# One stage for the first output projection, the norm and the routing, with expert slots found on chip

## The chip, the cores and the metric

The kernel runs on one NeuronCore of a Trainium2 chip. The metric is the device time of one execution in microseconds (us). Three runs of the kernel before took 3424.74, 3426.91 and 3428.15 us; their median is 3426.91 us. Everything is float32.

## The reference, cut to what matters

The model has two blocks; the change lies in the first one, between its attention and its mixture of experts. `x` is 512 tokens by 1024 features.

```python
x = x + concatenate([out_na, out_dil, out_mem], -1) @ w_out          # the first output projection
t = rms_norm(x, g_ffn)                                               # norm before the experts
grp_logits  = t @ w_r1 + b_r1                                        # 4 groups
fine_logits = (t @ w_r2 + b_r2).reshape(n, 4, 8)                     # 8 experts in a group
grp_idx = argmax(grp_logits); grp_gate = softmax(grp_logits)[grp_idx]
top_val, top_idx = top_k(fine_logits[:, grp_idx], 2)
gate = grp_gate * softmax(top_val)
y[token] += gate * ((silu(t @ w1[e]) * (t @ w3[e])) @ w2[e])         # for both experts e of a token
x = x + y
```

There are 32 experts, each with two 1024 x 512 matrices and one 512 x 1024 matrix, 6 MB together. 512 tokens with two experts each make 1024 rows, 32 rows to an expert in the mean.

## The kernel before, in words

The program is a row of stages. In a stage each engine has a list of instructions of its own, ordered by semaphores, and a stage begins only when every engine has ended the one before it, its awaited DMAs included. The helper `link` in the routing puts a wait for each VectorE instruction behind it, so a chain of small operations runs one after the other.

The stages around the change are, in order:

- `project_out` (L1117), stage `out1`. For each of 4 tiles of 128 tokens TensorE multiplies 8 chunks by 2 halves of `first_w_out` (L1203) and VectorE adds the bank to `x_rows` (L1263). Meanwhile SyncE asks for the weights of experts 0 and 1 (`experts.load_gate`, `load_up`, `load_down`, L239, L243, L247). The last of them, the down weights of expert 1, waits for the end of the products, since the attention's output lies in its place.
- `load_tiles` (L930), stage `in_ffn`: the norm weights, once by feature and once as a row copied to all partitions.
- `norm_and_turn` (L960), stage `norm_ffn`: squares and sums (L1017, L1052), root (L1021), inverse (L1063), scaled rows (L1027, L1068), 32 transposes (L1100), copies with the norm weights (L1036, L1077) into `hT`, the rows times the weights (L1086), and their store to the DRAM tensor `scr_tokens` (L1003).
- `route` (L1771). SyncE loads the router weights and constants (L1825) and then 17 tiles for the filter work described below (L1827). TensorE makes 36 logits a token (L1835). VectorE picks the group and the two experts in a chain of small operations (L1893 to L1923, the sum of the two one-hot choices is `both`). TensorE counts the earlier rows of each expert (L1843) and all rows (L1847). VectorE turns that into a slot number a row (L1951 to L1959), and GpSimd scatters the row's information to the DRAM tensor `scr_slot_info`, 8 indirect DMAs one after the other (L1977). An expert owns 64 slots; rows beyond 64 go to further blocks.
- `experts_stage` (L2333), stage `moe`. SyncE reads the slot table back (L2367). For each expert GpSimd gathers 64 rows from `scr_tokens` (L2322), TensorE transposes them (L2288), ScalarE copies the transposed rows (L2457), TensorE makes both up products (L2298), ScalarE and VectorE the gated activation (L2474, L2497), TensorE the down product (L2315), VectorE copies it (L2488) and GpSimd scatters the rows (L2329). SyncE asks for the gate weights of expert b + 2 when the first up product of expert b is done (L239), for its up weights when the second is done (L243), and for the down weights of b + 1 when the down product of b - 1 is done (L247). Two experts' weights fit on chip.
- Between these products runs `FilterWork` (L2009), which makes the spectra of long filters that a later layer needs. A fixed plan gives each of its pieces one of three slots an expert (`SLOTS`, `HID0`, `SUMS` and others), and every engine runs its part of the piece at that slot.
- `rest_stage` (L2503) computes the blocks beyond the first 64 rows of an expert, if there are any, and `combine_experts` (L2734) adds the gated rows to `x_rows`.

The order on VectorE in `experts_stage` is: filter piece 3b, the activation of b, filter piece 3b + 1, the copy of the down product of b - 1, filter piece 3b + 2. On ScalarE the copy of the transposed rows stands behind the SiLU:

```python
nc.scalar.activation(act1[:], ph1[:, 0:HF], ACT.Silu).then_inc(s_silu, 1)
filters.on_scalar(act, nc.scalar, n_slots * b)
if b + 1 < E:
    copy_x(b + 1)
```

## Time and profile before

| | |
|---|---|
| median of 3 runs | 3426.91 us |
| the profiled execution's own time | 3431.24 us |
| its span, first to last instruction | 3429.5 us |
| TensorE busy | 3035.7 us, 89% of the span |
| VectorE, ScalarE, GpSimd busy | 31%, 21%, 5% |
| mean granted TensorE clock | 0.947 of full |
| moved by DMA | 442.48 MB |
| stage `out1` begins | 461.8 us |
| stage `moe`: first DMA asked for, last product ends | 597.65 us, 1168.0 us |

Times in the rows are us from the start of the span. In a row of the timeline the first number is the start, the second the duration, and the bracket says how long the engine was idle before and what released it. PE is TensorE's matmuls, PEld its weight loads, DVE VectorE, ACT ScalarE, POOL GpSimd, SPq the queue of DMAs that SyncE issues. A float32 matmul of the program shows as two records, a transpose as one.

### The profile page before, as it was taken

The page shows a single profiled execution, that of the slowest core. Times are in us where ns is not written, and L with a number is a line of the kernel's source. Part 1 is how long each engine was busy: PE and PEld are TensorE (multiplying, and loading weights), DVE is VectorE, ACT ScalarE, POOL GpSimd, SP SyncE. Part 2 cuts the span into 40 slices and gives each one's busy share as a digit, 9 for nine tenths or more (in the row PEclk, how much of TensorE's full clock was granted, in tenths as well). Part 3 has the DMA queues.
Part 4 walks back from the last instruction along what each step waited for, and adds up shares of the span by engine and source line. Part 5 has one row for each costly group of instructions (what it writes and reads, how often), then busy time and mean ns, then how long its engine had stood idle before and what let it go on. Part 6 is the DMA issues. An engine that isn't in the chain of part 4 may idle for free. (4 is left out here: it accounts for less than half of the span.)

```text
span 3429.5 us, 34727 instructions
## 1 busy us (share of the span) xinstructions
PE 3035.7 (89%) x13906; PEld 1814.0 (53%) x13906; DVE 1051.1 (31%) x2186; ACT 732.2 (21%) x1603; POOL 164.3 (5%) x265
## 2 busy tenths in 40 slices
PE   6999993899899589899989899989997776888998
PEld 3448653555444275567545566445654343454674
DVE  3441623212211210125421037333311872201242
ACT  2111621111010020234220048310001110202441
POOL 0000000111011000000000002001110001000000
PEclk9999995899999899999999999999999887999999
DMA  6664344899999801120001220012224213011200
GB/s 217 239 227 169 136 172 119 309 387 389 386 391 387 315 19 49 37 74 1 25 0 37 62 87 2 1 55 86 88 88 142 74 62 122 0 55 52 71 1 25
DMA packets 246599, 442.48 MB, mean 129 GB/s; under 512 B 31503, under 2 KB 113439, under 8 KB 243116
## 3 DMA queue, kind: packets, MB, share of 16 engines
q1 hardware_dynamic: 234150, 403.96, 33.5%
q0 software_dynamic: 9776, 22.18, 1.9%
q10 hardware_dynamic: 2518, 14.16, 1.0%
q8 instruction: 110, 1.80, 0.2%
q14 instruction: 45, 0.37, 0.0%
HBM read 410.04 MB, written 37.81 MB: 131 GB/s over the span
## 5 line engine op out<-in xcount | busy, mean ns | idle before, releaser
L352 PE MATMUL hyena_in_main<-hT,weight_slots 128*128 128x256 f32 (+1 forms) x1024 | 330.5, 486 | 1.4 <-PEq L993 1.4
L352 PEld LDWEIGHTS hyena_in_main<-hT,weight_slots 128*128 128x128 f32 x1024 | 194.5, 190 | 137.2 <-issue 124.0
L2298 PE MATMUL moe_ph<-expert_weights,moe_x_T 128*64 128x256 f32 x2048 | 239.8, 388 | 23.9 <-DMA expert_weights<-w 15.0
L2298 PEld LDWEIGHTS moe_ph<-expert_weights,moe_x_T 128*64 128x64 f32 x2048 | 145.8, 139 | 133.1 <-issue 44.8
L352 PE MATMUL swa_in_main<-hT,weight_slots 128*128 128x512 f32 (+1 forms) x576 | 190.8, 491 | 6.8 <-DMA weight_slots<-b_w_in 5.4
L352 PE MATMUL mla_down_main<-hT,weight_slots 128*128 128x512 f32 (+1 forms) x448 | 168.5, 539 | 19.5 <-DMA weight_slots<-a_w_in 19.5
L1412 PE MATMUL qkv_main<-hT,weight_slots 128*128 128x512 f32 (+1 forms) x384 | 167.8, 580 | 0.9 <-PEq L993 0.9
L1203 PE MATMUL post_y<-expert_weights,hT 128*128 128x512 f32 x384 | 165.1, 592 | 0.0
L352 PEld LDWEIGHTS swa_in_main<-hT,weight_slots 128*128 128x128 f32 x576 | 110.4, 192 | 87.6 <-issue 74.7
L352 PE MATMUL mla_up_main<-expert_weights,weight_slots 128*128 128x512 f32 (+1 forms) x416 | 146.4, 511 | 2.8 <-PEq L993 2.4
L352 PEld LDWEIGHTS mla_down_main<-hT,weight_slots 128*128 128x128 f32 x448 | 88.1, 198 | 100.0 <-issue 75.0
L1203 PE MATMUL post_y<-expert_weights 128*128 128x512 f32 x320 | 137.7, 592 | 0.0
L2315 PE MATMUL moe_py<-expert_weights,moe_act_T 128*64 128x512 f32 x512 | 118.6, 606 | 4.5 <-DMA expert_weights<-w 4.5
L1203 PEld LDWEIGHTS post_y<-expert_weights,hT 128*128 128x128 f32 x384 | 73.0, 190 | 92.0 <-issue 92.0
L1412 PEld LDWEIGHTS qkv_main<-hT,weight_slots 128*128 128x128 f32 x384 | 71.1, 190 | 92.4 <-issue 85.8
L860 DVE TENSOR_REDUCE mla_att_stat<-mla_att_scores 128x1 f32<-128x768 f32 (+1 forms) x80 | 68.1, 851 | 165.7 <-PE mla_att_scores L802 154.3
L1473 DVE RECIPROCAL expert_weights<-expert_weights 128x512 f32<-128x512 f32 (+1 forms) x24 | 77.3, 3220 | 133.6 <-ACT expert_weights L1446 133.6
L352 PEld LDWEIGHTS mla_up_main<-expert_weights,weight_slots 128*128 128x128 f32 x416 | 78.8, 190 | 69.7 <-issue 64.5
L352 PE MATMUL mla_down_main<-weight_slots,hT 128*128 128x256 f32 x512 | 111.0, 379 | 2.8 <-PEq L993 2.8
L786 PE MATMUL mla_att_scores<-mla_kn,expert_weights 128*128 128x512 f32 (+1 forms) x288 | 107.1, 490 | 3.0 <-ACT weight_slots L900 1.5
L1217 ACT ACTIVATE post_squares<-post_y 128x512 f32<-128x512 f32 x44 | 26.3, 598 | 372.2 <-PE post_y L1203 371.5
L352 PEld LDWEIGHTS mla_down_main<-weight_slots,hT 128*128 128x128 f32 x512 | 97.1, 190 | 16.3 <-issue 3.2
(361 smaller groups left out, 4101.5 us busy)
## 6 DMA issues: line engine op xcount, KB each, us to landing
expert_weights<-w SPq DMA_DIRECT2D x96, 2048.0 KB, 21.8
first_w_out<-w_mod SPq DMA_DIRECT2D x12, 2048.0 KB, 8.1
expert_weights<-w_mod SPq DMA_DIRECT2D x12, 2048.0 KB, 8.1
weight_slots<-w_in SPq DMA_DIRECT2D x16, 1024.0 KB
weight_slots<-c_w_in SPq DMA_DIRECT2D x16, 1024.0 KB
weight_slots<-a_w_in SPq DMA_DIRECT2D x14, 1024.0 KB
expert_weights<-scr_spectra SPq DMA_DIRECT2D x12, 1024.0 KB, 4.9
weight_slots<-b_w_in SPq DMA_DIRECT2D x10, 1024.0 KB
```

The source lines that it names most:

```text
L352: mm = pe.matmul(main[u][0:unit.rows, 0:unit.cols], lhsT, rhs, start=(c == 0), stop=(c == r.kc - 1))
L786: mm = pe.matmul(region[e][:, b0:b1], qn[:, 2 * it.pair + e, it.q], kn[:, 2 * it.pair + e, it.first + b0:it.first + b1], start=start, stop ...
L860: nc.vector.tensor_reduce(sm[:, MX, e:e + 1], region[e][:, 0:it.keys], AX.X, ALU.max)\
L1203: mm = pe.matmul(y[k % 4][:, half * BANK:(half + 1) * BANK], z_T[:, c, s.at + t * P:s.at + (t + 1) * P], w_sb[:, c, half * BANK:(half + 1) ...
L1217: nc.scalar.activation(junk[:], y[k % 4][:, half * BANK:(half + 1) * BANK], ACT.Square, accum_out=stat[:, k, half:half + 1]).then_inc(s_sq, 1)
L1412: mm = pe.matmul(main[n % B][:, 0:u.cols], lhsT, rhs, start=(c == 0), stop=(c == KD - 1))
L1473: nc.vector.reciprocal(rt, rt).then_inc(s_inv, 1)
L2298: mm = pe.matmul(bank[half * T:(half + 1) * T, 0:HF], x_T[:, c, :], w[:, c, half * HF:(half + 1) * HF], start=(c == 0), stop=(c == KD - 1))
L2315: mm = pe.matmul(py[half * T:(half + 1) * T, :], act_T[:, c % per, c // per * T:(c // per + 1) * T], w[:, c, half * BANK:(half + 1) * BANK ...
```

## The change

The stages `out1`, `in_ffn`, `norm_ffn` and `route` become one stage, `front`:

- TensorE: after the products of tile k come the transposes of tile k - 1 and the logits of tile k - 2. VectorE adds tile k, ScalarE squares and sums it, takes the root, VectorE inverts it, and the two scale one half of the row each; both copy half of the transposed rows.
- The norm weights are no longer applied to the rows. They are multiplied once into the router weights, and in the expert stage into the gathered rows as these are copied. The row copy of the norm weights and the stage that loads it are gone.
- The slot table in DRAM is gone for the 32 own blocks. A one-hot matrix of slot numbers (128 rows by 128 slots, for each of 8 tile and choice pairs) is multiplied with the one-hot expert choices times the row's number, which gives each slot its row: `expert_slots` on chip. The 8 indirect DMAs and the table move to `rest_stage`, inside its branch.
- GpSimd gathers the rows of experts 0 and 1 in the new stage, into one tile of 128 partitions whose halves take turns.
- SyncE's order is: 13 constants, gate and up weights of experts 0 and 1, 9 filter tiles, the four stores of `scr_tokens`, down weights of expert 1, down weights of expert 0 (its place holds the scaled rows until they are stored).
- 8 filter tiles (3.8 MB: two halves of `filter_w`, the lag row, the decay table, four cosine and sine tables) are now asked for at the start of `experts_stage`, ahead of the weights of expert 2. The filter plan's `SUMS` moves from slot 3 to slot 6 and waits for them.
- In `experts_stage` the copy of the transposed rows moves from ScalarE to VectorE, with the norm weights as a second operand, between the activation and filter piece 3b + 1.
- The gates, the further blocks and their experts are computed after the slots are found.

Tiles that were allocated inside the second block are now allocated earlier, without other effect. The core of the diff:

```diff
+    def gather(self, pool, b):
+        at = slice(b % 2 * SLOTS_B, (b % 2 + 1) * SLOTS_B)
+        gather_rows(pool, self.rows[at, :], self.tokens, self.index[0:SLOTS_B, b, 0:1]).then_inc(self.gathered[b % 2], 16)
...
+def out_and_route(nc, a, x, hT, routed, experts, consts, room, more, beside):
...
+                for tile, src in loads:
+                    sp.dma_start(tile, src).then_inc(s_in, 16)
+                for e in range(experts.EARLY):
+                    experts.load_gate(sp, e)
+                    experts.load_up(sp, e)
+                for tile, src in beside:
+                    sp.dma_start(tile, src).then_inc(s_beside, 16)
+                for k in range(XT):
+                    for half in range(2):
+                        sp.wait_ge(s_normed[half], k + 1)
+                    sp.dma_start(routed.tokens[k * P:(k + 1) * P, :], normed[:, k, :]).then_inc(s_tok, 16)
+
+                sp.wait_ge(s_y, XT)
+                experts.load_down(sp, 1)
...
+                sp.wait_ge(s_tok, 16 * XT)
+                experts.load_down(sp, 0)
...
+                for k in range(XT):
+                    if k >= 2:
+                        pe.wait_ge(s_x, k - 1)
                     for j in range(KD):
...
+                    mm.then_inc(s_y, 1)
+                    if k:
+                        turn(k - 1)
+                    if k >= 2:
+                        logits(k - 2)
+                logits(XT - 2)
+                turn(XT - 1)
+                logits(XT - 1)
 
                 pe.wait_ge(s_hot, 1)
...
+                pe.matmul(pre[:, 0:XT * E], consts["earlier"][:], flat, start=True, stop=False, skip_group_check=True)
+                for k in range(1, XT):
+                    mm = pe.matmul(pre[:, k * E:XT * E], consts["ones"][:], flat[:, 0:(XT - k) * E],
+                                   start=False, stop=(k == XT - 1), skip_group_check=True)
...
+                for k in range(2 * XT):
+                    pe.wait_ge(s_slot_hot, k // XT + 1)
+                    mm = pe.matmul(slot_of[:, 0:E], slot_hot[:, k, :], tagged[:, k, :], start=(k == 0), stop=(k == 2 * XT - 1))
...
+                link(tt(tagged, hots, c["result_no"].rearrange("p (k o) -> p k o", o=1).to_broadcast([P, 2 * XT, E]),
+                        ALU.mult))
...
+                link(v.tensor_reduce(rank, picked, AX.X, ALU.add))
...
+                    tt(slot_hot[:, at, :], slot_no, rank[:, at, :].to_broadcast([P, XT, P]), ALU.is_equal)\
+                        .then_inc(s_slot_hot, 1)
...
+                link(v.tensor_scalar(f["empty"], tag, 0.5, float(UNUSED), ALU.is_lt, ALU.mult))
+                link(v.scalar_tensor_tensor(f["base"], tag, -1.0, f["empty"], ALU.add, ALU.add))
+                link(v.tensor_scalar(f["second"], tag, X + 0.5, -float(X), ALU.is_gt, ALU.mult))
+                link(tt(f["token"], f["base"], f["second"], ALU.add))
+                v.tensor_copy(routed.index[:, :, 0], f["token"]).then_inc(s_index, 1)
...
-    HID0, SIN0, HID1, SIN1, SUMS, FIRST = 2, 4, 5, 7, 3, 9
+    HID0, SIN0, HID1, SIN1, SUMS, FIRST = 2, 4, 5, 7, 6, 9
...
-                with nc.allow_non_contiguous_dma(reason="an index a row, a block to a column"):
-                    for dst, src in loads:
-                        sp.dma_start(dst, src).then_inc(s_idx, 16)
+                filters.load(sp)
...
-                    if b + 1 < E:
-                        copy_x(b + 1)
...
+                def copy_x(b):
+                    dve.wait_ge(s_px, b + 1)
...
+                    nc.vector.tensor_tensor(x_T[b % 2][:], px[:].rearrange("p (c n) -> p c n", n=SLOTS_B),
+                                            routed.gain[:].rearrange("p (c o) -> p c o", o=1)
+                                            .to_broadcast([P, KD, SLOTS_B]), ALU.mult).then_inc(s_xT, 1)
```

## Rows read from the trace of the kernel before

**Rows 1.** The page's 40 slices of 85.7 us: tenths busy, GB/s moved

```profile
PE   6999993899899589899989899989997776888998
GB/s 217 239 227 169 136 172 119 309 387 389 386 391 387 315 19 49 37 74 1 25 0 37 62 87 2 1 55 86 88 88 142 74 62 122 0 55 52 71 1 25
```

**Rows 2.** Windows: stretch, length, busy us per engine (instructions), PEclk, DMA share, GB/s

```profile
517.00:546.80 29.80, 5.89 (x32) 5.26 (x32) 13.00 (x17) 8.82 (x12) 0.00 (x0) 0.65 0.42 158
...
585.40:597.65 12.25, 0.00 (x0) 0.00 (x0) 0.00 (x0) 0.00 (x0) 7.75 (x8) 0.50 0.02 1
...
616.50:1168.00 551.50, 520.33 (x3354) 274.29 (x3348) 115.31 (x181) 55.08 (x121) 59.41 (x60) 0.99 1.03 383
```

**Rows 3.** Waits of PE from 616 to 1168: us in total, times, longest

```profile
PE moe_ph L2298 <- DMA expert_weights<-w: 15.0, 10, 5.6
...
PE moe_py L2315 <- DMA expert_weights<-w: 4.5, 4, 1.8
PE moe_px L2288 <- DMA moe_x<-scr_tokens,moe_index: 3.3, 6, 0.9
```

**Rows 4.** Timeline of the last head, the output projection and the norm

```profile
441.25 1.09 PE L571 MATMUL heads_turned<-const_identity,ctx_rows_and_rope 128*128 128x128 f32 x8
...
461.81 20.41 PE L1203 MATMUL out_y<-first_w_out,expert_weights 128*128 128x512 f32 x47 [0.63 <-PEq L535]
...
475.82 1.22 DVE L1263 TENSOR_TENSOR x_rows<-out_y,x_rows 128x1024 f32<-128x1024 f32 x1 [17.45 <-PE out_y L1203]
...
517.02 1.22 DVE L1263 TENSOR_TENSOR x_rows<-out_y,x_rows 128x1024 f32<-128x1024 f32 x1 [12.51 <-PE out_y L1203]
...
526.32 1.06 ACT L1017 ACTIVATE norm_ffn_squares<-x_rows 128x1024 f32<-128x1024 f32 x1 [64.81 <-PEq L935]
```

**Rows 5.** Timeline of the routing and of the first expert

```profile
553.10 13.87 PE L1835 MATMUL route_logits<-route_w,hT 128*128 128x36 f32 x64 [15.15 <-DMA route_slot_info<-slot_info]
...
567.24 0.17 DVE L1893 TENSOR_REDUCE route_gmax<-route_logit 128x4 f32<-128x16 f32 x1
...
573.78 0.29 DVE L1923 TENSOR_TENSOR route_both<-route_hot 128x128 f32<-128x128 f32 x1
...
584.32 0.17 DVE L1959 CAST route_slots<-route_dest 128x8 int32<-128x8 f32 x1
...
597.65 2.00 SPq L2367 DMA_DIRECT2D moe_index<-scr_slot_info  x2
...
603.46 0.97 POOL L2322 DMA_INDIRECT moe_x<-scr_tokens,moe_index  x1 [8.17 <-DMA moe_index<-scr_slot_info]
...
606.60 3.67 PE L2288 MATMUL moe_px<-const_identity,moe_x 64*128 64x64 f32 x16 [24.57 <-DMA moe_x<-scr_tokens,moe_index]
...
616.55 0.37 SPq L239 DMA_DIRECT2D expert_weights<-w  x1
...
619.89 2.00 PE L2288 MATMUL moe_px<-const_identity,moe_x 64*128 64x64 f32 x16
```

**Rows 6.** Windows of the filter tiles' loads: stretch, length, PEclk, DMA share, GB/s

```profile
554.00:558.00 4.00, 0.50 0.98 346
558.00:570.00 12.00, 0.50 1.05 209
570.00:574.00 4.00, 0.50 0.97 273
```

**Rows 7.** Weight stream's start: window of 20 to 60 us into the experts

```profile
620.00:660.00 40.00, 39.23 (x274) 0.96 1.05 387
```

**Rows 8.** An expert's copy of the gathered rows, the next product, VectorE's price

```profile
664.89 0.60 ACT L2457 ACTIVATE moe_x_T<-moe_px 128x512 f32<-128x512 f32 x1 [6.94 <-PE moe_px L2288]
...
670.34 3.67 PE L2298 MATMUL moe_ph<-expert_weights,moe_x_T 128*64 128x256 f32 x32
...
L2241 DVE TENSOR_TENSOR hT<-moe_filter_banks,ctx_rows_and_rope 128x512 f32<-128x512 f32 x48 | 30.9, 686 | 50.0 <-PE moe_filter_banks L2160 50.0
...
L2213 DVE TENSOR_TENSOR filter_w<-filter_w,weight_slots 64x2048 f32<-64x2048 f32 x2 | 4.6, 2282 | 0.0
```

More of the change, by code:

```diff
@@ L67 @@
 class Stage:
[L71 removed]
+    POOLS = ((99, 166), (166, 232))
     turn = 0
@@ new lines, in out_and_route @@
+    with Stage(nc, "front") as st:
+        z_T, w_out = consts["z_T"], consts["w_out"]
+        normed = experts.W2_flat(0).rearrange("p (t n) -> p t n", n=D)
+        squares = hT[:, 0:XT, X:TOK]
+        w, b = more.tile(KD, R), st.sb("b", [P, R])
+        c = {k: more.tile(P) if k == "slot_no" else st.sb(k, shape)[:] for k, shape in ROUTE_CONSTS.items()}
+        sums, root, inv = (st.sb(k, [P, XT]) for k in ("sums", "root", "inv"))
+        t = {k: room.tile(XT, n) for k, n in dict(
+            logit=R, gmax=1, geq=E_GROUPS, gcand=E_GROUPS, gidx=1, ghot=E_GROUPS, gexp=E_GROUPS, gsum=1, ggate=1,
+            off=E_GROUPS, fine=E, v1=1, eq1=E, cand1=E, i1=1, fine2=E, v2=1, eq2=E, cand2=E, i2=1,
+            both=E, diff=1, ratio=1, one=1, p1=1, p2=1).items()}
+        hots, tagged, picked, slot_hot = room.tile(2 * XT, E), room.tile(2 * XT, E), room.tile(2 * XT, E), room.tile(2 * XT, P)
+        t["hot1"], t["hot2"] = hots[:, 0:XT, :], hots[:, XT:2 * XT, :]
+        rank, over_at, under = room.tile(2 * XT, 1), room.tile(2 * XT, 1), room.tile(2 * XT, 1)
+        found = {k: more.tile(E) for k in ("second", "empty", "base", "token", "row")}
+        jump = more.tile(E)
+        count, blocks, end = st.sb("count", [E, 1]), st.sb("blocks", [E, 1]), st.sb("end", [E, 1])
+        over, blocks_wide, ended = st.sb("over", [E, X // SLOTS_B]), more.tile(P)[0:E], st.sb("ended", [E, REST + 1])
@@ new lines, in logits @@
+                def logits(k):
+                    for half in range(2):
+                        pe.wait_ge(s_copied[half], k + 1)
+                    if k == 0:
+                        pe.wait_ge(s_w, 1)
+                    for j in range(KD):
+                        mm = pe.matmul(lg[:, k * R:(k + 1) * R], hT[:, j, k * P:(k + 1) * P], w[:, j, :],
+                                       start=(j == 0), stop=(j == KD - 1), skip_group_check=True)
+                    mm.then_inc(s_lg, 1)
+                pe.wait_ge(Stage.out_in, Stage.out_loaded)
@@ L2116, in begin, with load @@
         self.s_lag_in = st.sem("next_lag0_in")
+        self.s_loaded = st.sem("filter_constants_in")
+        self.n_loads = 16 * len(self.loads())
+    def load(self, sp):
+        for tile, src in self.loads():
+            sp.dma_start(tile, src).then_inc(self.s_loaded, 16)
     ARG_STEPS = 6
```

522 lines of the change are left out of this document (280 added, 242 removed).

## The prediction

> **What bounds the kernel now.** I read the page's slices first. TensorE is busy nine tenths nearly everywhere, but slices 6 and 7 (514 to 600 us) fall to 7 and 3 tenths, and right behind them the moved bytes stay at some 388 GB/s for six slices [rows 1]. So there is a gap, and then a stretch that runs at the pace of the DMAs.
>
> The windows by stage say the same. From 517 to 546.8 us TensorE works 5.9 us, and from 585.4 to 597.65 not at all; from 616.5 to 1168 it is busy 520 us, the DMA engines' share is 1.03 and 383 GB/s move [rows 2]. In that stretch TensorE waits 15.0 and 4.5 us for expert weights and 3.3 us for gathered rows [rows 3]. The busy share would point to TensorE, the waits to the weights: the product in front of a wait is late only because its weights are, and the queue never runs dry. I take the expert stage as a weight stream of fixed length. It begins when SyncE may ask for the gate weights of expert 2, at 616.55, behind the first up product [rows 5]. All that the change saves is then how much earlier this request comes, less what is put in front of the stream.
>
> The timeline gives the path to that request. Products begin at 461.81 and the last tile is added from 517.02 [rows 4]; then norm, logits from 553.10 to 567.0, a VectorE chain from 567.24 to 584.5, eight scatters, the table read back from 597.65, a gather from 603.46 to 606.60, transposes, a copy, the first up product [rows 5]. From first product to request: 616.55 - 461.81 = 154.7 us.
>
> **The same path after the change, term by term.**
>
> 1. *Products.* Unchanged, 517.02 - 461.81 = 55.2 us [rows 4].
> 2. *Work put between them.* Before the products of tile 3 end, TensorE also runs two groups of 8 transposes and one group of logits. Eight transposes take 1.1 us [rows 4]. A group of logits is 16 records; at the low clock 64 took 13.87 us, 3.5 a group, and at the full clock 16 records of the same kind of weight load took 2.0 [rows 5]. TensorE will be at the full clock here, as it comes from long products, so 2.0; both ends go to the range. Sum 4.2 us.
> 3. *Tile 3.* VectorE's add 1.2 and ScalarE's squares 1.1 [rows 4], and I put 1.0 for accumulator read, root, inverse and their hand-overs, 0.6 for scaling half a row (half the elements of the add or the square). ScalarE then scales before it copies its half of tile 2, another 0.6 (a 512-wide copy) [rows 8]; TensorE does the logits of tile 1 meanwhile and then waits for that copy to do those of tile 2 (2.0), transposes tile 3 (1.1), waits for a 512-wide copy on VectorE (0.7) [rows 8] and does the last logits (2.0). Sum 10.4 us.
> 4. *Choice of group and experts.* From 567.24 to the end of `both` at 574.07 is 6.8 us [rows 5]. Two small operations leave the chain (-0.4), and one add of all logits comes before it (+0.4), with 0.2 for the hand-over: 7.0 us.
> 5. *From `both` to the comparison with slot numbers.* TensorE does 8 records of counts and 8 of prefixes, where it now has 20 of prefixes and 8 of counts. The engine has been idle by then for 7 us; at such a place the clock is at the low level (0.50) [rows 2], so 0.22 us a record [rows 5], a bit less for the narrow counts: 2.5 us. VectorE then needs two products of 128 elements (0.3 each), a sum over 256 (0.45) and the first comparison of 512 (0.69) [rows 5, 8]. The second comparison lies beside the slot products: 16 records at 0.22 = 3.5 us. With hand-overs 8.0 us.
> 6. *Slots to indices.* Five operations of 32 columns, each near 0.17 and 0.04 behind it [rows 5]: 1.1 us. Here the two gathers may start: 3.1 us from issue to use [rows 5]. They are hidden behind term 7.
> 7. *Rest of the chain.* Index column, jumps, further blocks, gates: some 23 small operations of VectorE with one trip to ScalarE and back, 5.4 us by the same 0.2 each and a few of 256 elements at 0.45. Before, the gates lay beside TensorE's prefixes; now the stage's end waits for all of them. The next stage starts 0.3 us later, 461.81 against the end of the one before. Sum 5.7 us.
> 8. *First expert.* Transposes to request now take 616.55 - 606.60 = 9.95 us [rows 5]. The copy is 0.69 in place of 0.60 [rows 8]: 10.1 us. The clock is low at the start as before.
>
> Sum: 55.2 + 4.2 + 10.4 + 7.0 + 8.0 + 1.1 + 5.7 + 10.1 = 101.7 us. The request comes 154.7 - 101.7 = **53.0 us earlier**. In these 53 us lie the DRAM table (584.5 to 603.5, 19 us), the wait for the norm weights and the stage bounds, and most of the norm and the logits.
>
> **Queues that work is moved past.** SyncE issues 13 constants before the weights; the first up products come 90 us later, so this costs nothing. The four token stores stand behind 8 MB of weights and 1.1 MB of filter tiles, some 25 us of traffic; the last store is asked for only at about 525, when that is done. The two down weights follow, 4 MB or 11 us, over by about 540. If all that were late it would be the gather that waits, at 548.
>
> **What is put in front of the stream.** Eight filter tiles, 3.8 MB, are asked for as the expert stage begins. Before, they shared 20 us with a further megabyte of filter tiles, part at 346 GB/s, part at 209 although the engines' share was 1.05, part at 273 [rows 6]. By place in the queue the decay table (1.5 MB) is the fast part, the 64-partition halves of the filter weights (2.1 MB in all) the slow one, of which now 1.05 MB are left, and the tables the third (1.3 MB). So 4.3 + 5.0 + 4.6, about 13.5 us, from 1.5 us into the stage: done 15 us in. The weights' traffic would otherwise begin at 10.1 + 1.7 = 11.8 us in (their first bytes come about 1.7 us behind the request). The stream is at its full rate from its start [rows 7], so the 3.2 us are lost to it. All at 209 GB/s would be 18 us and 8 lost; if they slip into gaps, none. I take 3.2.
>
> **The move of the copy to VectorE** adds 32 x 0.69 = 22 us to 115 of 551 us [rows 2]. I cost it at nothing: VectorE has ended the activation, 0.4 us behind the second up product, when the transposes (2.0 us) end, and the copy is not wanted before the down product is over: 670.34 - 665.49 = 4.9 us of room at a typical expert [rows 8]. What stands behind it on VectorE, a filter piece and the copy of the down product, waits for TensorE anyhow. If that cover is gone, TensorE loses what the copy is later than 4.9 us. ScalarE loses 19 us of work, which frees nobody.
>
> A rule speaks against such a move. The Trainium skill, "SBUF — State Buffer", section "SBUF: two separate sides", says that a two-port VectorE operation locks GpSimd out of writing descriptors. By it the gathers would be late and the waits of rows 3 would grow. Its page "VectorE: DVE Perf Modes", "Why PSUM operands drop a tier", excludes PSUM operands from that mode, and this copy reads PSUM. No run here shows either yet.
>
> For the logits the skill's "TensorE: Matmul & The Clock Gate", section "LDWEIGHTS", gives columns / 1.2 ns, an estimated 1.7 us a group, not the 2.0 taken; by it the forecast would be about 1 us lower.
>
> **The sum.** 53.0 - 3.2 = 49.8 us gain. The profiled execution took 3431.24 us; 3431.24 - 49.8 = 3381.4. The median of the runs shown is 4.3 us below that execution, so the forecast for the median is **3377 us**.
>
> **The rivals.**
>
> *A. Less gain.* The terms come out at their dear ends: all logits at the low clock (+6, of which some 5 on the path), the filter tiles at 209 GB/s (+5), the tile pipeline of term 3 and the tail some 2 longer. Gain 38, time 3389. For it: the small loads' rates [rows 6]. Against: the clock was full through the products. Chance 0.24.
>
> *B. More gain.* TensorE's clock stays high to the slot products (24 records at half the price, -2.5), the filter loads find gaps (-3.2). Gain 55.5, time 3371. Against: the low clock between sparse products [rows 2]. Chance 0.16.
>
> *C. Slower.* The copy on VectorE becomes the link of the expert loop: VectorE stands in its order at a filter piece or the activation when the transposes end. Price: over 31 experts it has to eat 49.8 us and 7 more, 1.8 us each, so the copy must end 6.7 us behind today's. It decides from 4.9 us on. At 6.9 us late the time is 3377 + 31 x 2.0 = 3439. For it: filter work of up to 4.6 us in one go [rows 8]. Against: this comes once or twice, and VectorE is busy a quarter. Chance 0.02.
>
> *D. No change.* The stream isn't what ends the stage, or the rows beyond 64 slots exist after all and the table is still made (here no instruction of that stage shows, and the choice is computed as before). Then part of the gain is lost; all of it only if something unseen holds the stage's end, 3427. Chance 0.02.
>
> **How the numbers follow.** The forecast's own case, gain 45 to 54, has 0.56. A and B lie on the same side. The range goes from B with a further 5 us of earlier stream, 3366, to A with 4 us more, 3393; beyond it lie C, D and the tails of A and B, under 0.2. A change of 0.2% (7 us) is about what a measurement of this kernel can tell from none. Faster by more than that: 0.56 + 0.24 + 0.16 = 0.96; within: D, 0.02; slower: C, 0.02.
>
> **What the profile after should show.** Right: last tile added near 521; last logits ending near 531.5; indices near 548; first gather issued there; first transposes of the expert stage near 553.5; request for expert 2 near 563.5; down product of the last expert ending near 1118; the DMA share at 1.03 to 1.04 in between and stage `moe` from that request on 3 us longer than 551.5. Wrong: if TensorE's waits for expert weights grow to tens of us with a share below 1.0, the stream isn't the bound; if waits for VectorE's `moe_x_T` appear at each expert, C; if the stage from its request to the end is shorter by more than a few us, I misread the bound.

## The result, and the profile after

The changed kernel takes **3378.43 us** (median of 4 runs, 3378.07 to 3378.99) against 3426.43 us of the kernel before in the same comparison: 48.0 us less, ratio 0.986 (95% interval 0.9846 to 0.9874). Its profiled execution has its own time of 3378.07 us and a span of 3376.4 us. The forecast was 3377 us with a range of 3366 to 3393.

The page's slices of the changed kernel (the same two lines as [rows 1], slices of 84.4 us):

```profile
PE   6999997999999488999989999989997776888998
GB/s 219 235 236 164 150 180 208 385 385 390 388 389 385 183 44 38 35 66 1 26 13 47 54 76 2 1 74 88 87 90 140 63 84 103 13 44 53 72 1 25
```

The one slice at 3 tenths (514 to 600 us before) is one at 7 now, and its neighbour has 9 instead of 8. The stretch at 385 to 390 GB/s begins one slice sooner; before, it was five slices at 386 to 391 with partly filled ones on both sides. It is as high as before: the stream has not become faster, it starts earlier.

Windows of the changed kernel (length, busy time per engine with instructions, granted clock, DMA share, GB/s), the front stage and then the stretch from the request for expert 2's gate weights to the end of the last down product:

```profile
517.00:546.80 29.80, 19.19 (x103) 16.88 (x102) 12.66 (x42) 4.53 (x7) 0.00 (x0) 0.63 0.44 159
566.30:1118.00 551.70, 523.66 (x3342) 275.26 (x3340) 136.27 (x212) 36.78 (x90) 58.66 (x60) 0.98 1.03 384
```

Beside [rows 2], TensorE works 19 of 29.8 us where it worked 5.9, and the expert stage has the same share and rate. VectorE is busy 136 us there instead of 115, ScalarE 37 instead of 55: the moved copy. TensorE's waits in the expert stage (us in total, times, longest), to be held against [rows 3]:

```profile
PE moe_py L2462 <- DMA expert_weights<-w: 11.1, 7, 1.8
PE moe_ph L2445 <- DMA expert_weights<-w: 8.0, 9, 1.3
...
PE moe_px L2436 <- DMA gathered_rows<-scr_tokens,expert_slots: 2.5, 3, 1.1
```

19.1 us for weights where there were 19.5, and 2.5 for gathered rows where there were 3.3. The waits are those of a stage that is still paced by its weights; the first group of experiments tests that.

Now the timeline. The last tile, from its add to the last logits:

```profile
519.63 1.23 DVE L1994 TENSOR_TENSOR x_rows<-front_y,x_rows 128x1024 f32<-128x1024 f32 x1 [12.95 <-PE front_y L1901]
...
520.30 1.87 PE L1891 MATMUL front_logits<-weight_slots,hT 128*128 128x36 f32 x16
...
523.94 2.90 PE L1891 MATMUL front_logits<-weight_slots,hT 128*128 128x36 f32 x16 [1.77 <-ACT hT L1939]
...
526.65 1.95 PE L1881 MATMUL front_turned<-const_identity,expert_weights 128*128 128x128 f32 x8
...
529.38 3.60 PE L1891 MATMUL front_logits<-weight_slots,hT 128*128 128x36 f32 x16 [0.78 <-ACT hT L1939]
...
533.02 0.31 DVE L2005 TENSOR_TENSOR ctx_rows_and_rope<-front_logits,front_b 128x144 f32<-128x144 f32 x1 [4.54 <-PE front_logits L1891]
```

The same group of 16 logits records takes 1.87, 2.90 and 3.60 us, and 8 transposes 1.95 instead of 1.04. The clock by windows says why: 1.00 from 519 to 523, 0.93 from 523 to 525, 0.50 from then on. Behind it, the chain to the slots, the gathers and the first expert:

```profile
539.90 0.42 DVE L2038 TENSOR_TENSOR ctx_rows_and_rope<-ctx_rows_and_rope,front_result_no 128x256 f32<-128x256 f32 x1
...
544.23 3.62 PE L1929 MATMUL front_slot_of<-ctx_rows_and_rope 128*128 128x32 f32 x16 [1.01 <-DVE ctx_rows_and_rope L2056]
...
548.79 0.18 DVE L2064 CAST expert_slots<-weight_slots 128x32 int32<-128x32 f32 x1
...
549.97 1.37 POOL L2469 DMA_INDIRECT gathered_rows<-scr_tokens,expert_slots  x1 [507.44 <-DVE expert_slots L2064]
...
551.64 0.96 POOL L2469 DMA_INDIRECT gathered_rows<-scr_tokens,expert_slots  x1 [0.30 <-issue]
...
553.92 0.24 DVE L2098 TENSOR_TENSOR gates<-ctx_rows_and_rope 128x4 f32<-128x4 f32 x2
...
555.14 1.12 SPq L2261 DMA_DIRECT2D filter_w<-f_w  x2
...
555.34 3.64 PE L2436 MATMUL moe_px<-const_identity,gathered_rows 64*128 64x64 f32 x16 [4.91 <-PEq L1851]
...
559.76 10.02 PE L2445 MATMUL moe_ph<-expert_weights,moe_x_T 128*64 128x256 f32 x64 [0.78 <-DVE moe_x_T L2618]
...
566.37 0.37 SPq L244 DMA_DIRECT2D expert_weights<-w  x1
```

**Where the gain sits.** Counted from the first product (460.88 us here, 461.81 before) the request for expert 2 comes at 105.5 us instead of 154.7: 49.2 earlier. From the request to the start of the last down product it is 550.9 us (1117.27 - 566.37) instead of 547.8: 3.1 given back. So the last down product starts 46.2 us sooner. By stretches, read from the first two rows of the table below: from the last add to the last logits it is 36.6 us less, from the last logits to the first gather (choice, slots, and the DRAM table before) 19.5 less; the last add itself comes 3.5 later, and from first gather to request it is 3.3 more, since the gathers now lie ahead of the stage's bound, the point where one stage ends and the next begins. No run takes the DRAM table away alone, so its share is read from these marks and not tested.

The two profiled spans differ by 53.1 us; the first product starts 0.9 us sooner, and what lies behind the last down product took 6.0 less. Of these, 0.4 lie before the next norm, where the stage for further blocks and the combination stand; the 5.6 behind it, where the code is the same, are not credited to the change: all that lies behind the last down product took from 2255 to 2262 us in the kernels below.

### The profile page after: what moved, and what is told of

The parts are those of the page before. It is cut to its first block and busy times, and to the rows that moved or that the text cites. A ratio compares the mean times of both kernels' runs of the same rounds, so it can differ in the third digit from the quotient of the medians.

```text
span 3376.4 us, 34713 instructions
## 1 busy us (share of the span) xinstructions
PE 3034.6 (90%) x13910; PEld 1808.9 (54%) x13910; DVE 1067.7 (32%) x2219; ACT 716.4 (21%) x1580; POOL 156.3 (5%) x256
## 5 line engine op out<-in xcount | busy, mean ns | idle before, releaser
L2462 PE MATMUL moe_py<-expert_weights,moe_act_T 128*64 128x512 f32 x512 | 126.3, 638 | 11.1 <-DMA expert_weights<-w 11.1
L2590 ACT ACTIVATE moe_act_T<-moe_pa 128x256 f32<-128x256 f32 x32 | 12.3, 384 | 469.3 <-PE moe_pa L2453 469.3
```

Source lines behind the costliest of these rows:

```text
L2462: mm = pe.matmul(py[half * T:(half + 1) * T, :], act_T[:, c % per, c // per * T:(c // per + 1) * T], w[:, c, half * BANK:(half + 1) * BANK ...
L2590: nc.scalar.activation(act_T[:].rearrange("p c n -> p (c n)"), pa[:, 0:HF], ACT.Copy)\
```

## The experiments

Total times carry this spread of the later stages, so an edit worth a few us is read by its marks: us from the first product of the front stage (or of the output projection before), in each kernel's profiled execution. "Moe" is from the request to the last down product.

| kernel | last add | last logits end | first gather | first transposes | request | last down product | moe |
|---|---|---|---|---|---|---|---|
| before | 55.2 | 105.2 | 141.7 | 144.8 | 154.7 | 702.6 | 547.8 |
| changed | 58.8 | 72.1 | 89.1 | 94.5 | 105.5 | 656.4 | 550.9 |
| changed, again | 58.7 | 71.8 | 88.8 | 94.3 | 103.9 | 656.4 | 552.5 |
| f_late | 58.7 | 72.8 | 89.8 | 95.2 | 105.2 | 667.8 | 562.6 |
| gates_early | 58.7 | 72.1 | 89.1 | 94.4 | 105.5 | 656.1 | 550.7 |
| logits_again | 58.7 | 73.1 | 90.1 | 95.5 | 105.3 | 657.8 | 552.5 |
| both edits (best) | 58.8 | 72.0 | 89.0 | 94.3 | 103.8 | 656.3 | 552.5 |
| dense_fill | 58.8 | 70.8 | 87.9 | 91.9 | 103.0 | 656.6 | 553.6 |
| batch_order | 55.2 | 77.2 | 94.2 | 99.5 | 109.7 | 661.5 | 551.7 |
| gather_back | 58.8 | 71.7 | 94.4 | 103.6 | 113.7 | 662.6 | 548.8 |
| copy_scalar | 58.8 | 71.8 | 88.8 | 94.4 | 103.9 | 655.9 | 551.9 |

### Is the expert stage a stream, and what do the filter tiles take from it?

**f_late**: the filter tiles are asked for behind expert 2's up weights.

```diff
-                filters.load(sp)
                 for b in range(E):
...
                         experts.load_up(sp, b + 2)
+                    if b == 0:
+                        filters.load(sp)
```

> The eight filter tiles are asked for behind the gate and up weights of expert 2 instead of ahead of them; nothing else moves. Theory 1 (the expert stage is a weight stream whose queue never runs dry): the tiles' 13.5 us of traffic no longer use the 10 us in which the stage waits for its first product, so all of it lies in the stream: 3378.4 + 13.5 - 3.2 = 3389, a stage from request to the last down product of 561 us where the changed kernel has 550.9. Theory 2 (TensorE sets the stage's length, the weights are only just ahead of it): the time stays at 3378 within 2 us.

Measured: 3391.41 us (3388.67 to 3397.26), ratio 0.9898 (0.9881 to 0.9914). The request comes where it did, and the stage is 562.6 us, 11.7 longer than in the changed kernel, with 25.6 us of waits for weights:

```profile
PE moe_py L2462 <- DMA expert_weights<-w: 14.7, 11, 1.9
PE moe_ph L2445 <- DMA expert_weights<-w: 10.9, 12, 1.6
```

The last down product comes 11.4 us later than in either execution of the changed kernel. Against the second of them, the stage is 10.1 longer. The tiles cost nearly their whole traffic there; ahead of the request they go mostly beside the first expert. So the queue is the bound, and the order on it is worth some 11 us.

**fewer_bytes**: a quarter of each down weight of experts 2 to 31 isn't loaded.

```diff
-        sp.dma_start(self.W2[e % 2], self.w2[e]).then_inc(Stage.w2_in[e % 2], 16)
+        n = FF // P if e < self.EARLY else FF // P - 1
+        sp.dma_start(self.W2[e % 2][:, 0:n, :], self.w2[e][:, 0:n, :]).then_inc(Stage.w2_in[e % 2], 16)
```

> The down weights of experts 2 to 31 are loaded in three of their four chunks (the fourth keeps what an earlier expert left, so this part of the down products uses other weights): 30 x 0.52 = 15.7 MB less, at 384 GB/s 41 us less traffic. Theory 1 (weight stream): the stage gets shorter until TensorE has no waits for weights left; it has 19.1 us of them, so 17 to 22 us less, 3357 to 3361, and the DMA share falls below 1. Theory 2 (TensorE sets the length): 0 to 5 us less.

Measured: 3345.3 us (3342.69 to 3347.13), ratio 0.9758 (0.9742 to 0.9774). From request (566.87) to last down product (1082.54) 515.7 us, 35.2 less; no wait for weights is left. TensorE is then busy for all but 4 us of the stage at full clock. The first row is the changed kernel from its request to the end of its last down product, the second is this one over the same 3352 instructions:

```profile
566.37:1120.92 554.55, 526.51 (x3352) 275.98 (x3348) 136.27 (x212) 36.78 (x90) 59.11 (x60) 0.98 1.03 383
...
566.87:1086.19 519.32, 515.35 (x3352) 270.88 (x3348) 136.25 (x212) 36.79 (x90) 58.99 (x60) 1.00 1.03 380
```

30 quarters of 2.1 MB are 15.7 MB, at 386 GB/s 40.8 us: of these 35.2 came back, and then TensorE is the bound. I had expected half, the 19.1 us of waits, because I took TensorE's 520 us busy in [rows 2] for its own need. It is not: it is busy 526.5 us in the changed kernel (granted clock 0.98) and 515.4 here (1.00).

The second part of the expectation failed too: the DMA share did not fall below 1. It is 1.03 at 380 GB/s where no weight is waited for. So in this kernel the share doesn't tell whether the queue or TensorE sets the pace; the waits do. Without these bytes the two bounds lie close together: the stream alone would take 550.9 - 40.8 = 510 us, an estimate, and TensorE takes 515.

**pe_extra**: four of the eight transposes of each expert's rows are done twice.

```diff
-    for c in range(KD):
+    for c in (*range(KD // 2), *range(KD)):
         mm = pe.matmul(px[:, c * T:(c + 1) * T], x[:, c * P:(c + 1) * P], eye, start=True, stop=True)
```

> TensorE transposes the first half of each expert's gathered rows twice: 8 records, 1.0 us at the full clock, 32 times, 32 us more of TensorE. Theory 1 (weight stream): the 19.1 us in which TensorE waits for weights swallow part, the rest is added: 5 to 14 us more, 3383 to 3392. Theory 2 (TensorE sets the length): 32 us more, 3410.

Measured: 3390.46 us (3386.68 to 3394.3), ratio 0.9896 (0.9879 to 0.9912). The stage is 557.8 us, 6.9 longer, with no wait for weights left:

```profile
568.35:1129.83 561.48, 556.34 (x3600) 302.33 (x3596) 136.26 (x212) 36.79 (x90) 59.00 (x60) 0.97 1.02 378
```

From the request to the end of the last down product TensorE is busy 29.8 us more (556.3 against 526.5) and the stage is 6.9 longer: the other 23 us went into the waits that the stream had left it. Theory 2, TensorE as the bound, expected all 32. How far TensorE alone is from the stream can't be read to better than some 10 us, since its granted clock is 0.97 here and 1.00 in fewer_bytes.

### The wait for the norm weights, alone

**b_weights_early** is the kernel before with one edit: the norm weights are loaded in the stage of the output projection, and the stage that loaded them is gone.

```diff
-        project_out(nc, "out1", None, None, [Stream(x, XT, 0)], X, consts, experts=experts)
+        project_out(nc, "out1", None, None, [Stream(x, XT, 0)], X, consts, experts=experts,
+                    also=[(consts["g_ffn"], a["g_ffn"]), (consts["g_ffn_row"], a["g_ffn_row"].to_broadcast([P, D]))])
...
-            load_tiles(nc, "in_ffn", [(g[:], a["g_ffn"]), (row[:], a["g_ffn_row"].to_broadcast([P, D]))])
+            g, row = consts["g_ffn"], consts["g_ffn_row"]
```

> The kernel before with one part of the change alone: the norm weights are loaded in the output projection's stage, into a region that is idle there, and the stage that loads them is gone. Theory 1 (all that lies between the last product and the first request of the stream is on the path): the 8 us from the last tile's addition to the norm's first instruction go, 3426.4 - 8 = 3418. Rival (the down weights of expert 1, asked for at 517, were what the next stages waited for anyway): 2 us or less.

Measured: 3420.6 us (10 runs, 3415.61 to 3427.38), ratio 0.9975 (0.9966 to 0.9985). The norm's first instruction follows the last add by 1.5 us, where it took 9.3 [rows 4]:

```profile
517.37 1.23 DVE L1268 TENSOR_TENSOR x_rows<-out_y,x_rows 128x1024 f32<-128x1024 f32 x1 [12.51 <-PE out_y L1208]
518.89 1.06 ACT L1017 ACTIVATE norm_ffn_squares<-x_rows 128x1024 f32<-128x1024 f32 x1 [57.04 <-PEq L1154]
```

That is 7.8 us less. The logits begin 6.9 us sooner than before (84.4 us after the first product, 91.3 before), the request 6.7 (148.1 against 154.7) and the last down product 6.8 (695.8 against 702.6). The total is 8.7 below that of before in the same comparison, 3429.26; what it has beyond 6.8 lies in the spread of the later stages. So about a seventh of the 46.2 us of the change is this wait, and what is won at the request arrives whole at the last down product.

### What tile by tile is worth

**batch_order**: all products first, then the four tiles' transposes and logits (ScalarE's and VectorE's copies follow that order).

```diff
                     mm.then_inc(s_y, 1)
+                for k in range(XT):
+                    turn(k)
                     if k:
-                        turn(k - 1)
-                    if k >= 2:
-                        logits(k - 2)
-                logits(XT - 2)
-                turn(XT - 1)
+                        logits(k - 1)
                 logits(XT - 1)
```

> The tile by tile order of TensorE is undone: all output products first, and the transposes and logits of the four tiles behind them; the loads, the choice and everything later stay. Theory 1 (interleaving hides three tiles' transposes and two groups of logits, and costs 4.2 us before the last add): the last tile is added 3 to 4 us sooner, but the last logits end later, at the low clock some 3 to 8 us; total 3 to 8 us more. Rival (the interleaving hides little, since the norm of tile 3 is the path): within 1 us of the changed kernel.

Measured: 3386.96 us (3384.86 to 3388.51), ratio 0.9878 (0.9862 to 0.9894). The last add is 3.5 us sooner; the last logits end 5.1 later, the request comes 4.2 later and the last down product 5.1. The price of the order is in these rows (8 transposes and a group of logits, behind the last products at 516.1):

```profile
520.35 1.06 PE L1881 MATMUL front_turned<-const_identity,expert_weights 128*128 128x128 f32 x8 [3.37 <-DVE hT L1980]
...
521.25 3.40 PE L1891 MATMUL front_logits<-weight_slots,hT 128*128 128x36 f32 x16
```

All four groups of logits cost 3.4 us or more; tile by tile two of them ran at the full clock. This is 5 us of a gain of 48: the interleaving is a small part of the change. At the price of the full clock (1.87 a group) the four groups would cost some 6 us less than the 13.8 that they take here, an estimate that is more than the 5 us lost. So the clock may be the larger part of what the order is worth; no run held the clock high in this order.

### Why the last tile took 13.4 us

**logits_again**: in the gap before the logits of tile 2 TensorE repeats those of tile 1, with the same result.

```diff
-                    mm.then_inc(s_lg, 1)
+                    return mm
...
-                logits(XT - 2)
+                for k in range(1):
+                    logits(1)
+                logits(XT - 2).then_inc(s_lg, 1)
```

> TensorE repeats the logits of tile 1 in the gap where it waits for the copies of tile 2; the repeated result is the same and nothing else changes. Theory 1 (tile 3 took 13.4 us and not 10.4 because TensorE's clock fell to its low level in that gap, so that the last logits cost 3.6 us instead of 1.9): the group takes about 1.9 us in a gap of 1.8, the clock stays high, the later groups take 1.9, 1.0 and 1.9, and the last logits end 3.5 us sooner; total 3 us less. Rival (the clock falls anyway, or tile 3 is long because of the copies by ScalarE and VectorE): last logits end at the same time or up to 2 us later.

Measured: 3383.37 us (3378.74 to 3385.76), ratio 0.987 (0.9854 to 0.9887); last logits end at 73.1, 1.0 later than in the changed kernel. The theory as I wrote it falls: up to the moment of the fall TensorE had no gap, and lost its clock all the same. Two neighbouring windows (columns as above), with TensorE busy throughout:

```profile
523.00:524.00 1.00, 1.00 (x11) 1.00 (x10) 0.21 (x2) 0.74 (x4) 0.00 (x0) 1.00 0.00 0
...
525.00:526.00 1.00, 1.00 (x6) 1.00 (x7) 0.00 (x0) 0.15 (x1) 0.00 (x0) 0.50 0.47 188
```

**gates_early** and both edits together (**best**) belong to the next question; **dense_fill** takes up this one. It is the kernel with both edits, but what stands in the gaps are 512-wide products, and only one gather stays ahead of the stage's bound.

```diff
+                def dense(n):
+                    for i in range(n):
+                        pe.matmul(slot_of[:], consts["identity"][:], w_out[:, i, 0:BANK], start=True, stop=True)
...
-                for k in range(1):
-                    logits(1)
+                dense(4)
                 logits(XT - 2).then_inc(s_lg, 1)
                 turn(XT - 1)
+                dense(2)
                 logits(XT - 1).then_inc(s_lg, 1)
...
-                for b in range(2):
-                    routed.gather(pool, b)
+                routed.gather(pool, 0)
...
+                routed.gather(pool, 1)
                 for b in range(1, E):
```

> As the kernel with both edits, but what fills TensorE's gaps at the last tile is not logits: four 512-wide products into the bank of the slot products before the logits of tile 2, and two before the last logits (unread, overwritten later); and only the first gather stays ahead of the stage's bound, the second goes behind it. Theory 1 (at tile 3 the clock falls where no wide products come between transposes and logits, idle or not): the clock stays at 1.00 until the last logits end, these end 69 us after the first product instead of 72; rival (it falls at the same moment, some 5 us behind the last output product, whatever is done): they end at 72 to 74. Theory 1 for the bound (it waits 2.5 us behind GpSimd's last gather, not for VectorE): from the issue of the first gather to the first transposes of the expert stage 4.1 us instead of 5.3; rival (it waits for VectorE or for the gathered rows themselves): 5.3 as before. Both together: first transposes 90.2 us after the first product instead of 94.4, total some 4 us less than the changed kernel, 3374 to 3375 us; neither: 3379 us.

Measured: 3380.81 us (3376.23 to 3384.33), ratio 0.9859 (0.9843 to 0.9876). The clock is 1.00 in every window from 519 to 533 us. The first group of wide products and the last group of logits:

```profile
523.87 3.68 PE L1897 MATMUL front_slot_of<-first_w_out,const_identity 128*128 128x512 f32 x8
...
531.72 1.87 PE L1891 MATMUL front_logits<-weight_slots,hT 128*128 128x36 f32 x16
```

The last logits cost 1.87 instead of 3.60 us, and end at 70.8, not 69. The clock theory holds in its second form: narrow work, idle or not, let the clock fall here; wide products between kept it. The missing 1.8 us are my sizing: four products are 8 records, 3.68 us in a gap of 1.8, and the two before the last logits take 1.88 in one of 0.8. So 1.3 of about 3 us were had, and a filler that fits would be needed for the rest. That wasn't tried.

### What the end of the front stage waits for

**gates_early**: the block of operations on the gates stands before VectorE's wait for the slot products.

```diff
+                link(tt(t["gexp"], G, wide(t["gmax"], E_GROUPS), ALU.subtract))
...
                 dve.wait_ge(s_slot_of, 1)
...
-                link(tt(t["gexp"], G, wide(t["gmax"], E_GROUPS), ALU.subtract))
```

> Only the block of operations on the gates is moved on VectorE, from the end of the chain to the 3.1 us in which it waits for TensorE's slot products. Theory 1 (the front is one chain, its tail waits for every small operation, and an earlier request for weights is worth its full time): the stage ends 1.9 us sooner, request 103.6 us after the first product instead of 105.5, total 1.9 us less. Rival (the small operations of the gates lie beside other work, or the exponential's trip to ScalarE holds the comparison up): no gain, or up to 1 us more.

Measured: 3384.47 us (3380.71 to 3386.25), ratio 0.9875 (0.9858 to 0.9891). VectorE ends its chain 2.0 us sooner (91.3 instead of 93.3 us), and the next stage starts at the same moment. So VectorE isn't what the bound waits for. The total is 5 us above the changed kernel's 3379.41 in the same comparison, though the last down product comes at 656.1 us here and at 656.4 there: it is the later stages that took 2262 us here and 2256 there. I have no cause for that.

**best**: this, the repeated logits, and the operations on the experts' ends moved too.

> Both edits together, and the operations on the experts' ends are moved beside the slot products too. Theory 1: some 6 us less than the changed kernel, 3372 us, request 99.5 us after the first product. Rival (the two edits have the same cover, or a filter tile backlog takes the earlier start): 3376 us or more.

Measured: 3380.23 us (3375.65 to 3382.56), ratio 0.986 (0.9844 to 0.9877): no better than the changed kernel. VectorE's chain ends at 90.7, the first transposes are where they were.

The bound waits for **GpSimd's gathers**. From the end of the last gather's issue to the next stage's first DMA: 552.60 to 555.14 = 2.5 us in the changed kernel, 552.71 to 555.23 in gates_early, 553.34 to 556.01 in best. Where the gathers aren't ahead of the bound (gather_back, below), the next DMA comes 0.26 us behind VectorE's last operation (555.30 to 555.56). With one gather, in dense_fill:

```profile
550.64 1.15 POOL L2474 DMA_INDIRECT gathered_rows<-scr_tokens,expert_slots  x1 [506.56 <-DVE expert_slots L2086]
...
554.42 1.12 SPq L2266 DMA_DIRECT2D filter_w<-f_w  x2
```

551.79 to 554.42 is 2.6 us again, and from first gather to first transposes it is 4.0 us instead of 5.3, as expected.

No row shows GpSimd at work in these 2.5 us, but the landing of the gathered rows fills them. The view of the tile gives the time from issue to landing, for the last gather ahead of the bound in the changed kernel and for the one in dense_fill:

```profile
L2469 POOL DMA_INDIRECT gathered_rows<-scr_tokens,expert_slots x1: 961/961/961, 551.6 to 551.6; - x1
DMA to landing us min/median/max: 3.1/3.1/3.1
...
L2474 POOL DMA_INDIRECT gathered_rows<-scr_tokens,expert_slots x1: 1147/1147/1147, 550.6 to 550.6; - x1
DMA to landing us min/median/max: 3.5/3.5/3.5
```

551.64 + 3.1 = 554.74 and 550.64 + 3.5 = 554.14: the next stage's first DMA comes 0.4 and 0.3 us behind. In gates_early, best, copy_scalar and the changed kernel's second execution (landings 3.1 to 3.4 us behind the start of the issue) it is 0.3 to 0.4 us too, as it is 0.26 behind VectorE where no gather is open. So the bound comes when the last gather has landed. The rival in the expectation, the gathered rows themselves, was priced wrongly at 5.3 us: with one gather ahead of the bound the landing is earlier too.

**gather_back**: both gathers stand behind the bound.

```diff
-                for b in range(2):
-                    routed.gather(pool, b)
...
+                for b in range(2):
+                    routed.gather(pool, b)
                 for b in range(1, E):
```

> The first two gathers are put back into the expert stage, behind its bound. Theory 1 (they are hidden behind the rest of the VectorE chain, 5.2 us): the first transposes begin 3 to 4 us later in the stage, total 3 to 4 us more. Rival (the stage is set by something else): no change.

Measured: 3388.25 us (3386.26 to 3390.38), ratio 0.9882 (0.9865 to 0.9898). The first transposes come 9.1 us later than in the changed kernel, more than twice what I expected, for the gathers now stand among the filter tiles:

```profile
556.83 1.15 POOL L2467 DMA_INDIRECT gathered_rows<-scr_tokens,expert_slots  x1 [513.17 <-issue]
...
565.99 3.67 PE L2434 MATMUL moe_px<-const_identity,gathered_rows 64*128 64x64 f32 x16 [14.42 <-DMA gathered_rows<-scr_tokens,expert_slots]
```

9.2 us from issue to use, against 3.1 in [rows 5], when the filter tiles had been loaded by 574 us [rows 6]. Of the 8.2 us at the request only 6.2 arrive at the last down product: the filter tiles are through before the request comes, so the stream has nothing in front of it and takes 548.8 us, 1.0 more than before and 2.1 less than in the changed kernel. This is the backlog term from the other side.

### Does the copy on VectorE cost anything?

**copy_scalar**: the copy is a plain one on ScalarE, as in the kernel before; the norm weights are left out of it.

```diff
+                def copy_x(b):
+                    act.wait_ge(s_px, b + 1)
...
+                    nc.scalar.activation(x_T[b % 2][:].rearrange("p c n -> p (c n)"), px[:], ACT.Copy).then_inc(s_xT, 1)
...
-                def copy_x(b):
-                    dve.wait_ge(s_px, b + 1)
```

> The copy of the turned rows in the expert loop is a plain copy on ScalarE again, at its old place; it leaves out the product of the norm weights with the gathered rows. Theory 1 (the copy has cover on either engine): 0, within 0.5 us, VectorE's busy time in the expert stage back by 21 us. Rival (VectorE's copies are part of what TensorE waits for, or lock GpSimd out): 3 us or more less than the changed kernel, fewer waits for gathered rows.

Measured: 3380.96 us (3379.48 to 3382.55), ratio 0.9864 (0.9848 to 0.9881). VectorE is back at 115 us busy, ScalarE at 55:

```profile
565.70:1118.00 552.30, 521.02 (x3338) 274.69 (x3336) 115.34 (x181) 55.08 (x121) 58.27 (x60) 0.98 1.03 384
```

The last down product comes 0.5 us sooner than in the changed kernel. The copy costs nothing that can be told from the spread.

**after_again** is the changed kernel unaltered, as the measure for the kernels beside it.

> The changed kernel once more, unaltered, as the measure for the three edits beside it: 3378 us; last logits end 72 us after the front stage's first product, request for expert 2's weights 105.5 us after it.

Measured: 3379.41 us (3376.25 to 3380.18), ratio 0.986 (0.9843 to 0.9876). Its request comes 1.6 us sooner than in the first profile, since the first up product ran from the start of its products to the request in 5.2 instead of 6.6 us: the clock had risen by 564 in one (1.00 from 564 to 566) and not in the other (0.58). The last down product is at 656.4 in both. So the mark of the request is good to about 1.6 us. In six executions (changed, again, gates_early, best, dense_fill, copy_scalar) requests from 103.0 to 105.5 led to last down products within 0.7 us of each other. Here the prediction's rule, that a sooner request is worth its full time, stops being visible, and the backlog would explain it: the filter tiles still stand in front of the weights when the request comes, so 1 or 2 us at the request are not passed on. What then counts is when the tiles are asked for, at the start of the stage. logits_again fits that: its request is within the same bounds (105.3), but its stage starts 1.1 us later than that of the changed kernel (first transposes at 95.5), and its last down product comes 1.4 later. dense_fill doesn't: its stage starts 2.6 us sooner, and nothing is left of it. Up to 113.1 us behind the first product it has moved 6.16 MB in this stage (287 GB/s over 21.45 us), the changed kernel 5.49 (291 over 18.88), which at 386 GB/s is 1.7 us ahead. So the lead is lost later in the stage, and I can't say where.

## Why the prediction was right, step by step

The time was 1.4 us from the forecast and well inside the range. Its mechanism stands: the expert stage is a stream that starts with the request, and the gain is how much earlier that comes, less the backlog. Some of the precision is luck: the steps add up to 46.1 us in the profiles, not 49.8, and the time shown is 48.0; what that has beyond them is of the size of the later stages' spread.

The first paragraph of the prediction misread its slices. Only one of them, 514 to 600 us, is low, at 3 tenths, and the next has 8; behind it five slices run at 386 to 391 GB/s, not six [rows 1]. No term rests on this. Its reading of the DMA share as a sign of the stream was too strong as well: fewer_bytes has the same share with TensorE as the bound.

| step | predicted | measured |
|---|---|---|
| 1 and 2, first product to last add | 59.4 | 58.8 |
| 3, last tile | 10.4 | 13.4 |
| 4, choice | 7.0 | 7.0 |
| 5, to the slots | 8.0 | 7.9 |
| 6, indices | 1.1 | 1.1 |
| 7, rest of the chain and bound | 5.7 | 6.4 |
| 8, first expert to the request | 10.1 | 11.0 |
| sum | 101.7 | 105.5 |
| filter tiles in front of the stream | 3.2 | 3.1 |

*Steps 1 and 2* hold; transposes 1.04, logits 1.87 at full clock. The Trainium skill, "TensorE: Matmul & The Clock Gate", section "LDWEIGHTS", gave an estimated 1.7 us a group and I took 2.0: the row lies between them, and neither matters.

*Step 3* is the one that was mis-sized, by 3.0 us. I wrote that TensorE would be at the full clock, "as it comes from long products", and charged all of tile 3 at that level. That was true of the first group only; the fall cost 1.0 us in the logits of tile 2, 0.9 in the transposes and 1.7 in the last logits. That the work's kind and not the gap lets the clock fall was shown by logits_again and dense_fill. The low-clock case stood in rival A, so the range had it, but for all logits, not for those of the last tiles alone.

*Steps 4 to 6* came out to 0.1 us. They are sums of many small VectorE operations that had rows of the same shape.

*Step 7*: the chain itself ended 5.2 us behind the indices. The bound after it was 1.0 us and not 0.3, since it waits for the second gather's landing. I had called the gathers hidden; they are not quite, by 0.7 us. *Step 8*: 0.9 us over, in the first up product at the low clock; the same kernel did it in 9.6 us the second time, so this is spread between executions.

*Filter tiles*: 3.1 us against 3.2, and that close only by luck: in the changed kernel's second execution the same two marks give 4.7 (552.5 against 547.8), with the request sooner by as much. f_late (11.4 us more at the last down product when they go into the stream) and gather_back (the stage 2.1 us shorter when they are through in time) bear the mechanism out.

*The copy at nothing*: shown by copy_scalar; rival C is out. The rule of the Trainium skill, "SBUF — State Buffer", section "SBUF: two separate sides", would have had the gathers late. TensorE's wait for gathered rows was 2.5 and 3.4 us in two executions with the copy on VectorE, 2.9 in copy_scalar and 3.3 before, and a gather takes 0.95 us of GpSimd (median of 29) in the stage either way. So the waits did not grow. This agrees with the exception for PSUM operands that the prediction took from the Trainium skill, "VectorE: DVE Perf Modes", section "Why PSUM operands drop a tier"; a copy that reads SBUF wasn't tried, so the rule itself wasn't tested.

*Rival A* had one of its terms come true in part, the low clock; *rival B* had none. D is out.

**What to carry to other kernels.** When a stage is paced by a queue of loads, measure a change ahead of it by when the first request goes out and by what stands in front of it in the queue, and don't count on the last 1 or 2 us arriving. Charge short, narrow TensorE work behind a long product at both clock levels, and look for the moment of the fall in the granted clock: filling the gap with more narrow work didn't help here. Before moving operations off the engine that ends last at a stage's bound, look at all engines and at the transfers that they have open: here the landing of GpSimd's last gather held the bound, and not VectorE.

## What the runs showed of the hardware

- TensorE's granted clock went from 1.00 to 0.50 at about 525 us though the engine was busy without a gap from the last wide products up to the fall (logits_again), and stayed at 1.00 to 533 with wide products between (dense_fill).
- A stage's bound came 2.5 to 2.8 us behind the end of the last gather's issue, and 0.3 to 0.4 us behind its landing, in six executions; it came 0.3 us behind VectorE where no gather was open.
- A gather of 64 rows took 3.1 us from issue to use on a quiet queue and 9.2 us among the filter tiles, whose traffic ran at 218 GB/s from 558 to 562 us there with the DMA share at 0.99.
- A busy TensorE isn't a measure of its need: 526.5 us busy, at a granted clock of 0.98, for instructions that take 515.4 at 1.00 when no weights are late. Nor is the DMA share a measure of the queue's part: 1.03 in both.
